# Input stage of a hybrid diffusion block: modulation products in fp32 on four column tiles over raw weights, with shift and scale panels alternating and h made by quarters

## The chip, the cores and the metric

The kernel runs on one core of one Trainium2 chip. The metric is the device time of one execution in microseconds (us). A core has a matrix engine (TensorE, PE in the rows; its weight loads are PEld), VectorE (DVE), ScalarE (ACT), GpSimd (POOL), and SyncE (SP), which here only issues transfers. ACT issues transfers as well, on a queue of its own.

## What is computed

A layer with two token mixers and a feed-forward part, on 256 context and 256 latent tokens of width 2048. Only its beginning matters here:

```python
mod_x = jax.nn.silu(c) @ lp['ada_w'] + lp['ada_b']        # ada_w: 2048 x 12288
mod_c = jax.nn.silu(c_ctx) @ lp['ada_w'] + lp['ada_b']
shx1, scx1, gx1, shx2, scx2, gx2 = [t[:, None, :] for t in jnp.split(mod_x, 6, axis=-1)]
shc1, scc1, ... = jnp.split(mod_c, 6, axis=-1)
hx = rms_norm(x, lp['norm_pre_mix']) * (1.0 + scx1) + shx1
hc = rms_norm(ctx, lp['norm_pre_mix']) * (1.0 + scc1) + shc1
px = hx @ lp['w_in']; pc = hc @ lp['w_in'][:, :MIX_IN]
```

The stage in question makes the first two of the six parts (shift and scale, 4096 columns of ada_w, 32 MB) and from them hx and hc. The other four parts are added up during the next stage, on DVE.

## The kernel before, in words

The program is a row of phases, each closed by a barrier that also clears semaphores (end_phase, L89). The first, phase_inputs (L282), ends with h ready; the second, phase_w_in (L618), multiplies h by w_in.

**Layout.** h is kept features-major, 16 feature tiles of 128 partitions by 512 tokens (context first), as two float32r parts: h_hi is h rounded, h_lo the rest. Modulation values are in modv, one column for each feature tile and each of the two vectors.

**Weights.** ada_w comes in 32 tiles of 1 MB (4 row blocks of 128 by 512 columns, sources of 2 KB each), 4 tiles to a panel of 512 columns, 8 panels. Panels 0 to 3 are the shift, 4 to 7 the scale, and they are taken in that order. raw holds four tile slots (RAW, L60). A Ring (L155) handles each tile: ACT rounds it to the high part (split_hi, L193), DVE (even tiles) or POOL (odd tiles) subtracts to get the low part (split_lo, L199), and PE multiplies both. SP loads a tile into a slot when the low part of the tile four earlier is there (L177).

**Products.** The stationary operand c_split holds silu(c) and silu(c_ctx), rounded and rest, in 4 of 128 columns, zeros in the others (L349, L388, L492, L545). The tile is the moving operand: eight products of 128x512 a tile (L473), all on the full array, added into one PSUM row block. When a panel is done, DVE copies four rows out (row, L562), PE turns them into columns with a small selector and sums the two parts (columns, L460; sel, L391), DVE copies the columns to modv (L564). Two panels make one loop body; the first two bodies are peeled, since they hold the other work.

**Other work of the stage, around the first tiles.** Four token blocks of 1 MB are loaded (L405, L417: the two x blocks reuse the ctx blocks' room), transposed on PE (turn, L434) and copied out by DVE (evac, L530). The parameters come as 25 small transfers on SP, between the ctx blocks and the first weight tile (L408), and are transposed (L448) and copied (L535). ACT stores x (L501) and squares (L504), PE adds the squares with a matrix of ones in plain fp32 (L442), DVE and ACT make 1/std (L550, L508, L552), DVE normalises in four quarters (L556).

**End of the stage.** After the last panel, DVE adds the bias to all of modv (L586), makes all gains (L589, L590), and then h is made for 16 feature tiles: ACT writes h_hi (L514), DVE the same in full into hbuf (L598), and DVE (even) or POOL (odd) subtracts (low, L365). SP prefetches the first four w_in tiles when all splits are done (L182).

Elsewhere, the scan phase has plain fp32 products of 64x64 on tiles of the array at row and column offset 0 or 64 (place, L1318; L1674, L1736, L1738).

Of the kernel before, what the change touches and what calls it, by code (L numbers as in the profile page):

```python
# [281 lines left out]
def phase_inputs(nc, A, env):  # L282
    alloc, psum, sem, Ring, col = (env[k] for k in ("alloc", "psum", "sem", "Ring", "col"))
# [3 lines left out]
    tile_no, bodies = env["tile_no"], env["bodies"]  # L287
# [27 lines left out]
    s_xt = [sem(f"i_tokens_landed{n}") for n in range(2)]  # L315
# [5 lines left out]
    s_std = sem("i_std_ready")  # L321
    s_nrm = sem("i_normalised")
# [3 lines left out]
    s_chi = sem("i_c_hi")  # L326
    s_clo = sem("i_c_split")
    s_rowc = sem("i_ada_row_copied")
    s_modp = sem("i_ada_columns_made")
    s_modc = sem("i_ada_columns_copied")  # L330
    s_v = sem("i_vector_step")
# [3 lines left out]
    s_gain = sem("i_gain_ready")  # L335
    ada = A["ada_w"].rearrange("a (k p) n -> p (a k) n", p=P)
    CW = 512
    siluc = env["siluc"]
    NB = LATE * P // CW // 2

    with ExitStack() as st:

        ring = Ring(st, "i", env["raw"], prefetched=False,
                    parts=[h.rearrange("p k t -> p (k t)").rearrange("p (s n) -> p s n", s=RAW)
                           for h in (h_hi, h_lo)])
# [3 lines left out]
        c_split = alloc(st, "c_split", [P, KT, P], f32r)  # L349
        sigc = alloc(st, "sigc", [P, 2 * KT])  # L350
        sel = alloc(st, "sel", [4, 2])
        sq = env["late_acc"][:].rearrange("p (k t) -> p k t", k=KT)
        rstd = alloc(st, "rstd", [P, TOK])
        hbuf = alloc(st, "hbuf", [P, 2, TOK])
        rows = alloc(st, "ada_rows", [4, 2, CW])
# [11 lines left out]
        tokens = [A["ctx"][0, 0:P, :], A["ctx"][0, P:2 * P, :], A["x"][0, 0:P, :], A["x"][0, P:2 * P, :]]  # L367

        with nc.Block() as block:

            @block.gpsimd
            def _(pool):
                made = [0]

                def make(ins):

                    made[0] += 1
                    ins.then_inc(s_const, 1)
                    pool.wait_ge(s_const, made[0])
# [4 lines left out]
                make(pool.memset(ones[:], 1.0))  # L384
                make(pool.memset(head_ones[:], 0.0))
# [3 lines left out]
                make(pool.memset(sel[:], 0.0))  # L389
                for base in (0, -2):  # L390
                    make(pool.affine_select(out=sel[:], in_=sel[:], compare_op=ALU.not_equal, fill=1.0, base=base,  # L391
                                            pattern=[[-1, 2]], channel_multiplier=1))

                def body(i):
                    for m in range(1, 8, 2):
                        ring.split_lo(pool, m, tile_no(i, 8, m))
                bodies(pool, NB, body, False)
                pool.wait_ge(ring.used, 8 * NB)
                for k in range(1, KT, 2):
                    low(pool, k, s_hlo)  # L400

            @block.sync
            def _(sp):
                for n in range(2):
                    sp.dma_start(xt[:, n, :], tokens[n]).then_inc(s_xt[n], 16)  # L405
                sp.wait_ge(s_const, 1)
                for tile, row, n, w, src in pieces:
                    sp.dma_start(prow[row:row + n, tile, 0:w], src).then_inc(s_prow, 16)  # L408

                def body(i):  # L410
                    for m in range(8):
                        src = ada[:, 4 * (m % 4):4 * (m % 4) + 4, bass.ds((i * 2 + m // 4) * CW, CW)]
                        ring.load(sp, src, m, tile_no(i, 8, m), (4, CW))
                        if isinstance(i, int) and i == 0 and m == 1:
                            for n in range(2, 4):
                                sp.wait_ge(s_xT, 4 * (n - 1))
                                sp.dma_start(xt[:, n % 2, :], tokens[n]).then_inc(s_xt[n % 2], 16)  # L417
                bodies(sp, NB, body, True)
                ring.prefetch(sp, 8 * NB, *first_w_in(A))
                sp.wait_ge(s_xst, 16)  # L420

            @block.tensor
            def _(pe):
                pe.wait_ge(s_const, 11)

                def turn(n):

                    pe.wait_ge(s_xt[n % 2], 16 * (n // 2 + 1))
                    for g in range(4):
# [3 lines left out]
                        for f in range(4):  # L433
                            last = pe.transpose(p_xT[b % 2][:, f * P:(f + 1) * P],  # L434
                                                xt[:, n % 2, (4 * g + f) * P:(4 * g + f + 1) * P], ident[:])
                        last.then_inc(s_xT, 1)

                def square_sums(q):
# [4 lines left out]
                    last.then_inc(s_ss, 1)  # L443
                turn(0)
                turn(1)
# [4 lines left out]
                pe.wait_ge(s_clo, 1)  # L450

                def columns(r, h):

                    pe.wait_ge(s_rowc, r + 1)
                    if isinstance(r, int) and r == 0:
                        pe.wait_ge(s_prm, 1)
                    else:
                        pe.wait_ge(s_modc, r)
                    for f in range(4):
                        last = pe.matmul(p_col[:, 2 * f:2 * f + 2], rows[:, h, f * P:(f + 1) * P], sel[:],  # L460
                                         start=True, stop=True)
                    last.then_inc(s_modp, 1)

                def body(i):
                    for h in range(2):
                        for q in range(4):
                            m = 4 * h + q
                            if q == 2 and not (isinstance(i, int) and i == 0 and h == 0):
                                columns(i * 2 + (h - 1), 1 - h)
                            ring.wait_split(pe, m, tile_no(i, 8, m))  # L470
                            for part in (ring.hi, ring.lo):
                                for k in range(4):
                                    last = pe.matmul(p_row[h][:], c_split[:, 4 * q + k, :],  # L473
                                                     part[:, m % ring.S, k * CW:(k + 1) * CW],
                                                     start=q == 0 and k == 0 and part is ring.hi,
                                                     stop=q == 3 and k == 3 and part is ring.lo)
                            last.then_inc(ring.used, 1)
                            if isinstance(i, int) and i == 0:
                                if m == 1:
                                    turn(2)  # L480
                                    turn(3)
                                if 3 <= m < 7:
                                    square_sums(m - 3)
                bodies(pe, NB, body, True)
                columns(2 * NB - 1, 1)

            @block.scalar
            def _(act):
                act.wait_ge(s_prm, 1)
                act.activation(sigc[:], prm[:, COL["c"]:COL["c"] + 2 * KT], ACT.Sigmoid).then_inc(s_sig, 1)  # L490
                act.wait_ge(s_sc, 1)
                act.activation(c_split[:, :, 0:2].rearrange("p k v -> p v k"), siluc[:], ACT.Copy)\  # L492
                   .then_inc(s_chi, 1)

                def body(i):
                    for m in range(8):
                        ring.split_hi(act, m, tile_no(i, 8, m))
                        if isinstance(i, int) and i == 0:
                            if m == 1:
                                act.wait_ge(s_fm, 16)  # L500
                                act.dma_start(xfm_d, fm[:, :, CTX:]).then_inc(s_xst, 16)  # L501
                            if 2 <= m < 6:
                                q = m - 2
                                act.activation(sq[:, 4 * q:4 * q + 4, :], fm[:, 4 * q:4 * q + 4, :], ACT.Square)\  # L504
                                   .then_inc(s_sq, 1)
                    if isinstance(i, int) and i == 0:
                        act.wait_ge(s_ssall, 1)
                        act.activation(rstd[:], rstd[:], ACT.Sqrt).then_inc(s_std, 1)  # L508
                bodies(act, NB, body, True)
                act.wait_ge(s_gain, 1)  # L510
                act.wait_ge(s_nrm, 4)
                for k in range(KT):
                    for v, lo in ((1, 0), (0, CTX)):
# [5 lines left out]
            def _(dve):  # L519
                step = [0]  # L520

                def done(ins):

                    step[0] += 1
                    ins.then_inc(s_v, 1)
# [2375 lines left out]
```

## Time and profile before

| | |
|---|---|
| median of 3 runs | 2608.91 us (2599.33 to 2609.03) |
| the profiled execution, its own time | 2605.06 us |
| its span, first to last instruction | 2603.0 us |
| busy over the span: PE, PEld, DVE, ACT, POOL | 85%, 72%, 57%, 33%, 17% |
| mean rate of all transfers over the span | 179 GB/s |
| phase_inputs, in the trace | 0 to 197.6 us |

The span is cut from the trace of one execution; the rest of its own time lies before the first and after the last instruction. Busy shares are unions of records, so records that overlap count once. A plain fp32 product leaves two PE records, a float32r product one. PEclk is the granted clock of TensorE, 1.00 for 2.4 GHz and 0.50 for 1.2 GHz.

### The profile page before, as it was taken

What the parts mean: (1) busy time and instruction counts of PE and PEld (TensorE: products, weight loads), DVE (VectorE), ACT (ScalarE), POOL (GpSimd) and SP (SyncE); (2) the same over time, 40 slices, a digit from 0 to 9 for tenths busy, and PEclk for the clock granted to TensorE, in tenths of its full rate; (3) what the DMA queues carried; (4) which work ended last, traced back from release to release, by engine and by line L of the source; (5) the groups of instructions that cost most, each with busy time, mean ns of one, the idle gap of its engine ahead of it and who ended that gap; (6) DMA issues with size and microseconds to landing.
All of it is one profiled execution on the core that took longest, in us unless ns stands there. A gap on an engine that the chain in (4) does not pass through costs nothing. (4 is left out here: it accounts for less than half of the span.)

```text
span 2603.0 us, 43450 instructions
## 1 busy us (share of the span) xinstructions
PE 2218.4 (85%) x18675; PEld 1883.0 (72%) x18675; DVE 1483.4 (57%) x1379; ACT 863.9 (33%) x878; POOL 451.2 (17%) x167
## 2 busy tenths in 40 slices
PE   6648999999799969957887839883999999989995
PEld 4437888887568857657887728773888888878884
DVE  3766666663337546667766567426655656554443
ACT  3453112111043225424433235323443333433331
POOL 3664222222103213300000014441000000000000
PEclk8778999999889989979999969996999999999996
DMA  8567888885064268854423056642555555555542
GB/s 293 183 205 273 314 314 297 319 313 139 15 194 105 77 181 276 269 110 85 76 53 75 4 196 200 202 161 96 181 192 181 189 182 189 177 194 192 197 154 105
DMA packets 438676, 465.71 MB, mean 179 GB/s; under 512 B 111822, under 2 KB 373182, under 8 KB 428798
## 3 DMA queue, kind: packets, MB, share of 16 engines
q1 hardware_dynamic: 429262, 450.23, 54.7%
q10 hardware_dynamic: 9264, 13.24, 1.4%
q8 instruction: 124, 2.03, 0.3%
q14 instruction: 26, 0.21, 0.0%
HBM read 417.69 MB, written 45.74 MB: 178 GB/s over the span
## 5 line engine op out<-in xcount | busy, mean ns | idle before, releaser
L254 PE MATMUL pf<-h,f_w_hi 128*128 128x512 f32 x1320 | 469.4, 398 | 0.0
L253 PE MATMUL pf<-h,f_w_lo 128*128 128x256 f32 x1320 | 370.2, 280 | 0.0
L199 DVE TENSOR_TENSOR f_w_lo<-t_w_raw,f_w_hi 128x2048 fp32r<-128x2048 f32 x88 | 201.4, 2289 | 173.6 <-ACT f_w_hi L193 173.6
L254 PEld LDWEIGHTS pf<-h,f_w_hi 128*128 128x128 f32 x1320 | 248.5, 188 | 56.9
L193 ACT ACTIVATE f_w_hi<-t_w_raw 128x2048 fp32r<-128x2048 f32 x88 | 168.6, 1917 | 299.1 <-PE pf L254 297.7
L253 PEld LDWEIGHTS pf<-h,f_w_lo 128*128 128x128 f32 x1320 | 249.6, 189 | 4.2
L254 PE MATMUL pd<-hid,h 128*128 128x512 f32 x688 | 244.8, 400 | 0.0
L193 ACT ACTIVATE p_w_hi<-h_w_raw 128x2048 fp32r<-128x2048 f32 (+1 forms) x54 | 98.0, 1862 | 409.1 <-DVE stage L741 252.2
L243 PE MATMUL p_in<-h,p_w_hi 128*128 128x512 f32 (+1 forms) x544 | 214.6, 395 | 19.8 <-DVE p_w_lo L199 19.8
L244 PE MATMUL p_in<-h,p_w_hi 128*128 128x512 f32 (+1 forms) x544 | 214.2, 394 | 0.0
L245 PE MATMUL p_in<-h,p_w_lo 128*128 128x512 f32 (+1 forms) x544 | 214.0, 393 | 0.0
L193 ACT ACTIVATE h<-t_w_raw 128x2048 fp32r<-128x2048 f32 x76 | 144.3, 1913 | 190.9 <-PE pd L254 150.3
L253 PE MATMUL pd<-hid,d_w_lo 128*128 128x256 f32 x688 | 193.8, 282 | 0.0
L199 POOL TENSOR_TENSOR p_w_lo<-h_w_raw,p_w_hi 128x2048 fp32r<-128x2048 f32 (+1 forms) x27 | 125.6, 4654 | 376.3 <-ACT p_w_hi L193 376.3
L871 DVE SCALAR_TENSOR_TENSOR late_acc<-h_of_x,siluc,late_acc 128x2048 f32<-128x2048 f32 x60 | 158.3, 2638 | 41.4 <-DMA h_of_x<-in_ada_w 39.8
L199 DVE TENSOR_TENSOR d_w_lo<-t_w_raw,h 128x2048 fp32r<-128x2048 f32 x44 | 100.2, 2291 | 106.6 <-ACT h L193 106.6
L254 PEld LDWEIGHTS pd<-hid,h 128*128 128x128 f32 x688 | 129.9, 189 | 31.6
L916 PE MATMUL r_pg<-h_of_x,gate_w 128*128 128x256 f32 x512 | 116.9, 386 | 20.2 <-PEq L92 12.0
L243 PEld LDWEIGHTS p_in<-h,p_w_hi 128*128 128x128 f32 (+1 forms) x544 | 100.7, 185 | 45.7 <-issue 21.3
L253 PEld LDWEIGHTS pd<-hid,d_w_lo 128*128 128x128 f32 x688 | 130.7, 190 | 0.8
L916 PEld LDWEIGHTS r_pg<-h_of_x,gate_w 128*128 128x128 f32 x512 | 99.2, 194 | 42.1 <-issue 28.6
L199 POOL TENSOR_TENSOR m_w_lo<-t_w_raw,h 128x2048 fp32r<-128x2048 f32 x8 | 40.2, 5031 | 472.6 <-ACT h L193 472.6
(438 smaller groups left out, 4486.7 us busy)
## 6 DMA issues: line engine op xcount, KB each, us to landing
h_of_x<-in_ada_w SPq DMA_DIRECT2D x64, 1024.0 KB, 5.2
h_w_raw<-in_w_in SPq DMA_DIRECT2D x48, 1024.0 KB, 7.6
t_w_raw<-in_ffn_w_gate SPq DMA_DIRECT2D x44, 1024.0 KB, 5.1
t_w_raw<-in_ffn_w_up SPq DMA_DIRECT2D x44, 1024.0 KB, 5.1
t_w_raw<-in_ffn_w_down SPq DMA_DIRECT2D x44, 1024.0 KB, 5.3
h_w_raw<-in_ada_w SPq DMA_DIRECT2D x32, 1024.0 KB, 5.7
gate_w<-in_w_in SPq DMA_DIRECT2D x32, 1024.0 KB, 5.8
t_w_raw<-in_w_out SPq DMA_DIRECT2D x16, 1024.0 KB, 5.5
```

What stands on the lines that cost most here:

```text
L193: act.activation(self.hi[:, m % self.S, 0:w], self.raw[:, s, 0:w], ACT.Copy)\
L199: eng.tensor_tensor(self.lo[:, m % self.S, 0:w], self.raw[:, s, 0:w], b32(self.hi[:, m % self.S, 0:w]), ALU.subtract)\
L243: pe.matmul(o, wh, xh, start=first, stop=False)
L244: pe.matmul(o, wh, xl, start=False, stop=False)
L245: return pe.matmul(o, wl, xh, start=False, stop=last)
L253: pe.matmul(hi, wl, x[:, 0, k, :], start=False, stop=False)
L254: return pe.matmul(both, wh, x[:, :, k, :], start=False, stop=last)
L871: dve.scalar_tensor_tensor(out=acc, in0=self.raw[:, t % 2], scalar=scalar, in1=acc, op0=ALU.mult, op1=ALU.add).then_inc(self.used, 1)
L916: mm = pe.matmul(self.banks[t % nb][:, 0:SEQ], self.raw[:, t % 2, k * P:(k + 1) * P], self.hx[:, k, :], start=k == 0, stop=k == KT - 1)
```

## The change

Products: c_cols holds the two silu vectors unrounded in 2 of 32 columns. Each of the four row blocks of a raw tile is multiplied in plain fp32 by its own 128x32 stationary block, with the output at partitions 0, 32, 64 or 96 of the same PSUM bank. Neither split is made, and a slot is free when its four products are done. The row copy takes all 128 partitions, and the selector (ones at 32g and 32g+1) adds the four groups.

Order: panels go 0, 4, 1, 5, 2, 6, 3, 7. Bias, gain and h are made for four feature tiles after each pair. All four token blocks are loaded at once (x into h_of_x), followed on SP by the weight tiles without the parameters; ACT issues the 25 parameter transfers. The w_in tiles are prefetched one by one as slots come free. PE does ctx block 0, parameters, ctx block 1, tile 0, x block 0, tile 1, x block 1, tiles 2 and 3, then a square sum after each of tiles 4 to 7; a panel's columns are made after the next panel's first tile.

```diff
-                make(pool.memset(b32(c_split[:]), 0.0))
+                make(pool.memset(c_cols[:], 0.0))
...
-                    for m in range(1, 8, 2):
-                        ring.split_lo(pool, m, tile_no(i, 8, m))
...
             def _(sp):
+                for n, (to, src) in enumerate(tokens):
+                    sp.dma_start(to, src).then_inc(s_xt[n], 16)
+                for t in range(TILES):
+                    if t >= RAW:
+                        sp.wait_ge(s_used, t - RAW + 1)
+                    at = panel(t // 4) * CW
+                    sp.dma_start(raw.slots[:, t % RAW].rearrange("p (k n) -> p k n", k=4),
+                                 ada[:, 4 * (t % 4):4 * (t % 4) + 4, at:at + CW]).then_inc(raw.landed[t % RAW], 16)
+                sources, shape = first_w_in(A)
+                for n, src in enumerate(sources):
+                    sp.wait_ge(s_used, TILES - RAW + 1 + n)
...
             def _(pe):
-                pe.wait_ge(s_const, 11)
+                pe.wait_ge(s_const, 3)
...
+                for t in range(TILES):
+                    p, q = t // 4, t % 4
+                    pe.wait_ge(raw.landed[t % RAW], 16 * (t // RAW + 1))
+                    for g in range(4):
+                        last = pe.matmul(p_row[p % 2][32 * g:32 * g + 32, :], c_cols[:, 4 * q + g, :],
+                                         raw.slots[:, t % RAW, g * CW:(g + 1) * CW], start=q == 0, stop=q == 3)
+                    last.then_inc(s_used, 1)
+                    if t < 2:
+                        turn(2 + t)
+                    if 4 <= t < 8:
+                        square_sums(t - 4)
+                    if q == 0 and p:
+                        columns(p - 1)
+                columns(PANELS - 1)
...
             def _(act):
+                act.wait_ge(s_const, 1)
+                for tile, row, n, w, src in pieces:
+                    act.dma_start(prow[row:row + n, tile, 0:w], src).then_inc(s_prow, 16)
...
                 for k in range(KT):
+                    if k % 4 == 0:
+                        act.wait_ge(s_nrm, k // 4 + 1)
+                        act.wait_ge(s_gain, k // 4 + 1)
...
             def _(dve):
+                row(0)
+                mod(0)
+                dve.wait_ge(s_ss, 4)
+                dve.tensor_scalar(rstd[:], p_ss[:], 1.0 / D, NORM_EPS, ALU.mult, ALU.add).then_inc(s_ssall, 1)
+                row(1)
+                dve.wait_ge(s_std, 1)
+                dve.reciprocal(rstd[:], rstd[:]).then_inc(s_rstd, 1)
...
+                normalised(0)
+                mod(1)
+                group(0)
+                for j in range(1, 4):
+                    normalised(j)
+                    row(2 * j)
+                    mod(2 * j)
+                    row(2 * j + 1)
+                    mod(2 * j + 1)
+                    group(j)
```

row(p) waits for the panel's last tile and copies PSUM to SBUF; mod(p) waits for the panel's columns and adds the bias into modv; normalised(j) scales a quarter of the tokens by 1/std; group(j) makes four gains and DVE's share of h for four feature tiles. columns(p) on PE waits for row(p) and mod(p-1).

## Rows read from the trace of the kernel before

**Rows 1.** Windows: busy us and instructions of each engine, granted clock, transfer share, GB/s
```profile
0.00:35.00 35.00, 19.36 (x83) 14.27 (x83) 13.61 (x23) 5.59 (x5) 8.60 (x16) 0.80 0.82 304
...
77.00:165.00 88.00, 63.75 (x228) 47.24 (x229) 67.38 (x28) 40.19 (x22) 67.70 (x12) 0.77 0.71 239
171.00:197.60 26.60, 0.00 (x0) 0.00 (x0) 23.25 (x44) 15.83 (x32) 10.77 (x8) 0.52 0.39 125
```
**Rows 2.** Waits of SP's own queue, 0 to 197.6 us: total, times, longest
```profile
SPq L179 <- DVE h L199: 72.0, 14, 16.7
SPq L179 <- POOL h L199: 51.9, 12, 6.1
```
**Rows 3.** Lines by form, 0 to 197.6 us: busy us, mean ns, idle before, releaser
```profile
L199 POOL TENSOR_TENSOR h<-h_w_raw,h 128x2048 fp32r<-128x2048 f32 x16 | 90.5, 5661 | 70.8 <-ACT h L193 70.7
L473 PE MATMUL p_row<-h,c_split 128*128 128x512 f32 x256 | 83.6, 484 | 31.8 <-DVE h L199 18.8 <-POOL h L199 13.0
L193 ACT ACTIVATE h<-h_w_raw 128x2048 fp32r<-128x2048 f32 x32 | 60.7, 1908 | 61.6 <-DMA h_w_raw<-in_ada_w 30.9 <-PE p_row L473 15.6 <-DVE fm L530 15.0
L552 DVE RECIPROCAL rstd<-rstd 128x512 f32<-128x512 f32 x1 | 3.4, 3353 | 0.7 <-ACT rstd L508 0.7
```
**Rows 4.** Windows: many transfers queued (first), one or two at a time (second)
```profile
14.00:34.00 20.00, 11.07 (x44) 8.00 (x44) 6.85 (x13) 4.30 (x4) 4.53 (x1) 0.66 1.03 397
125.00:155.00 30.00, 26.28 (x98) 19.83 (x98) 19.59 (x10) 17.23 (x9) 25.36 (x6) 0.83 0.93 317
```
**Rows 5.** Transfers by issue, whole span: count, KB each, median us to landing
```profile
h_w_raw<-in_ada_w SPq DMA_DIRECT2D x32, 1024.0 KB, 5.7
```
**Rows 6.** Timeline: start, length in us; fp32 products on full array and 64x64 tiles
```profile
49.67 3.60 PE L442 MATMUL p_ss<-late_acc,ones 128*128 128x512 f32 x8
...
1198.67 0.31 PE L1736 MATMUL pa<-vt_f,s2t_f 64*64 64x64 f32 x4
1198.79 0.31 PE L1738 MATMUL pa<-u_f,s1t_f 64*64 64x64 f32 x4
```
**Rows 7.** Windows: a stretch of the scan phase, columns as in rows 1
```profile
1180.00:1200.00 20.00, 17.60 (x585) 17.27 (x582) 15.47 (x23) 8.77 (x17) 0.00 (x0) 1.00 0.38 70
```
**Rows 8.** Timeline: the opening of the stage
```profile
1.67 0.43 SPq L408 DMA_DIRECT2D prow<-in_norm_pre_mix  x1
...
10.82 0.30 SPq L408 DMA_DIRECT2D prow<-in_gla_norm_g  x1
...
13.50 0.55 DVE L535 COPY prm<-p_col 128x384 f32<-128x384 f32 x1
...
20.91 3.75 PE L473 MATMUL p_row<-h,c_split 128*128 128x512 f32 x8 [7.73 <-DVE h L199]
...
29.16 1.04 PE L434 MATMUL p_xT<-ident,xt 128*128 128x128 f32 x8
...
34.18 1.29 DVE L530 COPY fm<-p_xT 128x512 f32<-128x512 f32 x2 [0.15 <-PE p_xT L434]
```
**Rows 9.** Timeline: a tile at either clock, a quarter normalised, one panel's columns
```profile
77.47 3.78 PE L473 MATMUL p_row<-h,c_split 128*128 128x512 f32 x8 [5.32 <-DVE h L199]
...
101.92 2.28 DVE L556 TENSOR_TENSOR fm<-fm,rstd 128x2048 f32<-128x2048 f32 x1
...
110.43 1.05 PE L460 MATMUL p_col<-sel,ada_rows 4*128 4x2 f32 x8 [1.27 <-DVE ada_rows L562]
...
111.41 2.11 PE L473 MATMUL p_row<-h,c_split 128*128 128x512 f32 x8
```
**Rows 10.** Timeline: the end of the stage
```profile
169.04 0.68 DVE L562 COPY ada_rows<-p_row 4x512 f32<-4x512 f32 x1 [4.60 <-PE p_row L473]
...
171.76 0.74 DVE L598 TENSOR_SCALAR hbuf<-fm,gain,modv 128x256 f32<-128x256 f32 x2
...
195.16 1.26 POOL L365 TENSOR_TENSOR h<-hbuf,h 128x512 fp32r<-128x512 f32 x1 [1.60 <-DVE hbuf L598]
...
197.64 0.86 SPq L858 DMA_DIRECT2D h_of_x<-in_ada_w  x2
```

More of the change, by code:

```diff
@@ L314, in phase_inputs @@
     s_prm = sem("i_params_ready")
-    s_xt = [sem(f"i_tokens_landed{n}") for n in range(2)]
+    s_xt = [sem(f"i_tokens_landed{n}") for n in range(4)]
     s_xT = sem("i_tokens_transposed")
@@ L383, in _ @@
                                         pattern=[[-1, P]], channel_multiplier=1))
+                make(pool.memset(c_cols[:], 0.0))
                 make(pool.memset(ones[:], 1.0))
+                make(pool.memset(sel[:], 0.0))
+                for g in range(4):
+                    make(pool.affine_select(out=sel[:], in_=sel[:], compare_op=ALU.not_equal, fill=1.0, base=-32 * g,
+                                            pattern=[[-1, 2]], channel_multiplier=1))
                 make(pool.memset(head_ones[:], 0.0))
@@ L403, in _ @@
             def _(sp):
[L404 to L419, printed above, removed]
+                for n, (to, src) in enumerate(tokens):
[9 more added lines that the diff above has]
+                    sp.wait_ge(s_used, TILES - RAW + 1 + n)
+                    sp.dma_start(raw.slots[:, n].rearrange("p (k n) -> p k n", k=shape[0]), src)\
+                      .then_inc(raw.landed[n], 16)
                 sp.wait_ge(s_xst, 16)
@@ L443, in square_sums, with columns @@
                     last.then_inc(s_ss, 1)
+                def columns(p):
+                    pe.wait_ge(s_rowc, p + 1)
+                    pe.wait_ge(s_modc, p)
+                    for f in range(4):
+                        last = pe.matmul(p_col[:, 2 * f:2 * f + 2], rows[:, p % 2, f * P:(f + 1) * P], sel[:],
+                                         start=True, stop=True)
+                    last.then_inc(s_modp, 1)
                 turn(0)
-                turn(1)
                 pe.wait_ge(s_prow, 16 * len(pieces))
@@ L449, in _ @@
                 last.then_inc(s_prmT, 1)
[L450 to L483, printed above, removed]
@@ L495, in body @@
[L495 to L508, printed above, removed]
@@ L531, in evac @@
                                     p_xT[b % 2][:].rearrange("p (f t) -> p f t", f=4)).then_inc(s_fm, 1)
-                for b in range(8):
+                for b in range(4):
                     evac(b)
@@ L590, in _, with row @@
-                dve.tensor_tensor(gain[:], gain[:], col("norm_pre_mix", 0, KT).unsqueeze(2)
-                                  .broadcast_to([P, KT, 2]), ALU.mult).then_inc(s_gain, 1)
-                dve.wait_ge(s_gain, 1)
-                dve.wait_ge(s_nrm, 4)
-                for k in range(KT):
-                    if k >= 2:
-                        dve.wait_ge(s_hlo if k % 2 else s_hl, k // 2)
-                    for v, lo in ((1, 0), (0, CTX)):
-                        last = dve.tensor_scalar(hbuf[:, k % 2, lo:lo + CTX], fm[:, k, lo:lo + CTX],
-                                                 gain[:, k, v:v + 1], modv[:, k, v:v + 1], ALU.mult, ALU.add)
-                    last.then_inc(s_h, 1)
-                    if k % 2 == 0:
-                        low(dve, k, s_hl)
+                def row(p):
+                    dve.wait_ge(s_used, 4 * p + 4)
+                    if p >= 2:
+                        dve.wait_ge(s_modp, p - 1)
+                    dve.tensor_copy(rows[:, p % 2, :], p_row[p % 2][:]).then_inc(s_rowc, 1)
@@ new lines, in group @@
+                def group(j):
+                    dve.wait_ge(s_modc, 2 * j + 2)
+                    at = slice(4 * j, 4 * j + 4)
+                    dve.scalar_tensor_tensor(out=gain[:, at, :], in0=modv[:, KT + 4 * j:KT + 4 * j + 4, :], scalar=1.0,
+                                             in1=col("norm_pre_mix", 4 * j, 4).unsqueeze(2).broadcast_to([P, 4, 2]),
+                                             op0=ALU.add, op1=ALU.mult).then_inc(s_gain, 1)
+                    dve.wait_ge(s_gain, j + 1)
+                    dve.wait_ge(s_nrm, j + 1)
+                    for k in range(4 * j, 4 * j + 4):
+                        if k >= 2:
+                            dve.wait_ge(s_hlo if k % 2 else s_hl, k // 2)
+                        for v, lo in ((1, 0), (0, CTX)):
+                            last = dve.tensor_scalar(hbuf[:, k % 2, lo:lo + CTX], fm[:, k, lo:lo + CTX],
+                                                     gain[:, k, v:v + 1], modv[:, k, v:v + 1], ALU.mult, ALU.add)
+                        last.then_inc(s_h, 1)
+                        if k % 2 == 0:
+                            low(dve, k, s_hl)
```

133 lines of the change are left out of this document (51 added, 82 removed).

## The prediction

> **What bounds the kernel now.** The change touches only the first stage, which ends at 197.6 us, so I read that stretch first by windows [rows 1]. Nothing in it is full. In the long middle, 77 to 165 us, PE is busy 63.75 of 88 us, DVE and POOL about 67 each, and the transfers 0.71 at 239 GB/s. From 171 us on PE does nothing at all: DVE, ACT and POOL make h. So there are two parts: a ring whose members wait for one another, and a serial tail.
>
> The waits of SP's queue say what the ring turns on [rows 2]: SP stood 72.0 + 51.9 = 123.9 us waiting for DVE and POOL to finish a low part before it could reload a slot. The lines [rows 3] give the price of one tile on each engine: ACT 1.9 us, POOL 5.7, PE 8 x 0.48 = 3.9 at mixed clock. A slot is held through landing, ACT, DVE or POOL. The transfers could go faster: with many queued they moved 397 GB/s, with the ring's one or two at a time 317 [rows 4]. A tile (1.049 MB) takes 2.64 us at the first rate and 3.31 at the second.
>
> In the tail [rows 10] 171.76 to 196.42 us, 24.66 us, goes to 16 feature tiles of h, 1.54 each, with nothing beside it, and the next stage's first issue comes 1.22 us later. What follows the barrier should keep its length, so the stage's end moves the total one for one.
>
> **The change, part by part.**
>
> *Splits removed.* 32 ACT roundings and 32 subtractions go, and with them all of the 123.9 us of waits. This gains nothing directly; it leaves two candidates for the pace, the transfers (2.64 us a tile) and PE's new products.
>
> *Products.* Four plain fp32 products of 512 columns replace eight float32r ones. The square sums are such products on the full array: four of them are 8 records in 3.60 us [rows 6], the last record's own length 0.59 included, so one record follows the next in 0.43 us, and one after another four cost 8 x 0.43 = 3.44 us. Do products on different array tiles run beside each other? The scan phase shows 64x64 ones on two diagonal tiles: groups of 4 records begin at 1198.67 and 1198.79 us, 0.12 apart, 0.029 a record [rows 6]. A record of 64 columns would need 0.43 / 8 = 0.054 us if it ran alone, so the overlap is 1.8-fold. With two tiles that is also what one gets if the two records of a product follow each other on their tile, and only the second overlaps the first record of the next product. For four tiles this gives one record time per product, 4 x 0.43 = 1.72 us a tile of weights; full overlap would give 0.86, none 3.44. I take 1.72, the pattern that the scan's row fits. The scan's tiles differ in rows too, while here all four read the same 128 partitions, each its own data; no row shows that case, hence the range and a rival.
>
> The Trainium skill (TensorE: Matmul & The Clock Gate, section on packing small matmuls) gives 2.38x for three column tiles of 32. By that alone, an estimate, four products would cost 3.44 / 2.38 = 1.45 us, the opening below would be 2 us shorter, and the total 2538.
>
> *Clock.* At 1.2 GHz all this doubles: a tile before took 3.78 us at half clock and 2.11 at full [rows 9]. 64x64 products kept 1.00 in the scan with PE busy 17.6 of 20 us [rows 7]. If the clock dropped at a transfer-bound pace, a tile would cost 3.44 us, PE would be busy all the time, and by the scan's row it should come back. I take full clock.
>
> *Start.* SP issues four token blocks and four tiles at once, 8.4 MB, 21 us at 397 GB/s. The 25 parameter transfers, 1.67 to 11.12 us on SP [rows 8], move to ACT's queue, but share the transfer engines with those 8.4 MB. Tile 0 needs silu of c, which needs them. Not delayed, they are copied at 13.5 us as before; behind everything, they land at about 25. I take 20, add 1.1 for transposing and copying and 3.5 for a token block, and start tile 0 at 24.6 us (before: 20.91 [rows 8]); both ends stay for the range, -5 and +5 us.
>
> *Opening, tiles 0 to 7.* PE does in order 8 tiles (8 x 1.72 = 13.8), two token blocks (29.16 to 35.47 less the last copy [rows 8], 2.8 each, 5.6), four square sums (4 x 3.60 = 14.4), one set of columns (1.05 [rows 9]). End: 24.6 + 34.9 = 59.4 us. Transfers are not the limit here, and storing x (2.1 MB, 5 us) fits in.
>
> *A new wait, in the middle.* DVE now does everything in order. After the square sums it needs about 5.2 us for 1/std (reciprocal alone 3.35 [rows 3]), then normalises a quarter (2.28 [rows 9]), makes bias and gain (0.4), a quarter of h (24.66 / 4 = 6.2), the next quarter's normalising (2.28) and row(2) (0.68): 59.4 + 17.0 = 76.4 us. PE reaches the columns of panel 2, after tile 12, at about 69.5 and stands there until 76.4. Queued behind that wait are tiles 13 to 16, whose slots fill meanwhile; then the transfers stop too. PE resumes at 77.5 and frees the first slot at 79.2. Later groups cost DVE 6.2 + 2.3 + 2 us in the 21 us of two panels: no such wait again, one of 1.5 us at most.
>
> *Steady run.* Tile 17, issued at 79.2, lands at about 84.2 (5.7 is the median with others in flight [rows 5]; alone I take 5). With three or four queued from here, 14 more tiles at 2.64 us: tile 31 lands at 121.2 and is used by 122.9. At 3.31 us a tile it would be 132.3. I take 397 GB/s, the row with as many queued.
>
> The Trainium skill (DMA: Bandwidth & Descriptors, specifications) puts HBM at about 358 GB/s a core, 2.93 us a tile; the total by that estimate would be 2544. The row's 397 over 20 us speaks against it.
>
> *End.* From the last product to h before: row 169.04, first h 171.76, 2.7 us, then one quarter, 6.2, and the barrier, 1.2: 10.1 us. The next stage begins at 133.0 us instead of 197.6. The four w_in tiles, issued as the last slots free, land until some 13 us after tile 31 (4 x 3.31), in time: the first is there before the stage begins, the last when its turn comes. POOL's share of h and its small work at the start lie beside DVE's.
>
> **Sum:** 197.6 - 133.0 = 64.6 us less. Against the profiled execution's own 2605.06 us: **2540**. That execution is 3.9 us under the median of 2608.91. Of the 64.6, 18.5 come from the tail (three quarters of 24.66), the rest from the ring.
>
> For this case alone the time lies between 2524 (full overlap, parameters early) and 2556 (317 GB/s, parameters late).
>
> **Rivals.**
>
> *Column tiles do not overlap,* since four streams would come out of the same 128 partitions; clock full. For it: no row shows that case. Against: the scan's 1.8. A tile costs 3.44 us and PE is the bound: opening 59.4 + 13.8 = 73.2, then 24 x 3.44 + 6 x 1.05 = 88.9, so 162.1, and with 10.1 the stage ends at 172.2, 25.4 us early: **2580**. The ring would gain little, the tail its 18.5.
>
> *Overlap as taken, but the clock stays at 1.2 GHz during these products.* 32 x 3.44 = 110.1, square sums 28.8, columns 16.8, token blocks 5.6, start 24.6: 185.9, end 196.0: **2603**, no change. Against it stands the scan's 1.00.
>
> *Slower: no overlap and half clock.* The place is L473's successor, the price 6.88 us a tile: 220.2 + 28.8 + 16.8 + 5.6 + 24.6 + 10.1 = 306.1 us, 108.5 later: **2714**. It decides from 4.2 us a tile on: (197.6 - 10.1 - 24.6 - 5.6 - 14.4 - 8.4) / 32. So even partly low clock, under 0.82 on average without overlap, makes it slower; in the middle of the ring it was 0.77 [rows 1], though there PE had gaps.
>
> *The change does not do what it says,* the splits going but the slot still waiting for something: only PE is left to wait for, which is the second case.
>
> **How the numbers follow.** Overlap and transfer-bound: 0.62. No overlap at full clock: 0.20. Overlap at half clock: 0.08. No overlap at low clock: 0.06. Something between the first two: 0.04. Faster by over 0.5% (13 us, about what can be told from no change here) is 0.62 + 0.20 + 0.04 = 0.86, same 0.08, slower 0.06. The predicted time is the likeliest case's. The range takes in that case with its bounds and the second with its own (the parameters' 5 us either way, 2575 to 2585): 2522 to 2586.
>
> **What would show it.** Right: four products a tile with PE records 0.43 us apart, two at a time; transfers near 1.0 share and 390 GB/s from tile 17 on; SP waiting for PE only; PE standing some 8 us for DVE's row(2) near 70 us; 6 us of h after the last columns; the second stage beginning near 133 us. Wrong: a tile of products at 3.4 us with PE busy throughout and SP waiting for it (no overlap), or granted clock 0.5 there; parameters landing well past 25 us; transfers at 0.9 share but 320 GB/s in spite of four slots; a second stage that is longer than before because its first tiles are late.

## The result and the profile after

| | before | after |
|---|---|---|
| median of 4 runs | 2608.97 us (2599.33 to 2610.39) | 2539.36 us (2537.36 to 2539.42) |
| ratio, 95% interval | | 0.974 (0.972 to 0.976) |
| the profiled execution, its own time | 2605.06 us | 2539.42 us |
| its span | 2603.0 us | 2537.6 us |
| first issue of phase_w_in | 197.64 us | 126.05 us |
| from there to the span's end | 2405.4 us | 2411.6 us |

69.6 us less. The prediction was 2540, 64.6 us under the profiled execution's own 2605.06, which lies 3.9 us under the median of before. The page of the kernel after, the span and the busy time of each engine:

```profile
span 2537.6 us, 43217 instructions
...
PE 2188.2 (86%) x18675; PEld 1836.9 (72%) x18675; DVE 1415.1 (56%) x1364; ACT 803.3 (32%) x845; POOL 365.1 (14%) x153
```

These shares hardly moved; the gain shows only in the stretch that the change touches. Windows of the kernel after: start and end, length, busy us of PE, PEld, DVE, ACT and POOL, granted clock, transfer share, GB/s.

```profile
15.00:35.00 20.00, 16.68 (x97) 9.32 (x98) 9.65 (x19) 4.67 (x4) 0.00 (x0) 1.00 0.99 344
35.00:50.00 15.00, 15.00 (x58) 5.98 (x57) 0.17 (x1) 4.15 (x3) 0.00 (x0) 1.00 1.06 402
65.00:75.00 10.00, 8.27 (x44) 3.50 (x44) 2.53 (x4) 0.00 (x0) 2.19 (x1) 0.58 0.56 187
80.00:110.00 30.00, 24.60 (x110) 6.78 (x102) 13.49 (x22) 4.21 (x9) 7.98 (x4) 0.51 1.04 387
```

Against the middle of the stage before, 239 GB/s [rows 1], the transfers are now the full resource (last row: 387 GB/s, 2.71 us a tile), except in a hole at 65 to 75 us. The 402 GB/s of the second row are not loads alone: 4.57 MB of loads and 1.46 MB of the store of x passed in those 15 us. Of the 24.66 us of h with PE idle at the end [rows 10] about a quarter is left. SP's waits, total, times, longest, show the ring:

```profile
SPq L405 <- PE p_row L458: 81.5, 27, 12.0
```

DVE and POOL [rows 2] are gone from it: a slot now waits for its products alone. Most of these 81.5 us are no loss, since SP waits for a slot while the other slots' transfers fill the queue; the hole at 65 to 75 us is the exception. The lines by form, 0 to 120 us: busy us, mean ns of one record, idle time before:

```profile
L458 PE MATMUL p_row<-h_w_raw,c_cols 128*32 128x512 f32 x256 | 45.7, 826 | 10.2 <-DMA h_w_raw<-in_ada_w 10.2
L442 PE MATMUL p_col<-sel,ada_rows 128*128 128x2 f32 x64 | 11.6, 304 | 9.8 <-DVE ada_rows L522 9.8
```

As many records as before, 256 [rows 3], each nearly twice as long (826 against 484 ns), and yet busy 45.7 instead of 83.6 us: they lie on top of one another. The timeline of the kernel after (start, length in us, records at the end of the line, wait before in brackets) shows the steps:

```profile
16.91 0.90 PE L448 MATMUL p_col<-ident,prow 128*128 128x128 f32 x3 [7.30 <-DMA prow<-in_gla_norm_g]
...
21.35 1.50 PE L458 MATMUL p_row<-h_w_raw,c_cols 128*32 128x512 f32 x8
...
25.41 1.07 PE L458 MATMUL p_row<-h_w_raw,c_cols 128*32 128x512 f32 x8
...
32.52 3.70 PE L434 MATMUL p_ss<-late_acc,ones 128*128 128x512 f32 x8 [0.70 <-ACT late_acc L479]
...
50.92 0.69 DVE L556 TENSOR_SCALAR rstd<-p_ss 128x512 f32<-128x512 f32 x1 [13.71 <-PE p_ss L434]
...
53.25 2.78 PE L458 MATMUL p_row<-h_w_raw,c_cols 128*32 128x512 f32 x24
57.04 1.06 PE L458 MATMUL p_row<-h_w_raw,c_cols 128*32 128x512 f32 x8 [1.01 <-DMA h_w_raw<-in_ada_w]
...
65.99 0.69 DVE L522 COPY ada_rows<-p_row 128x512 f32<-128x512 f32 x1
66.73 1.87 PE L442 MATMUL p_col<-sel,ada_rows 128*128 128x2 f32 x8 [8.62 <-DVE ada_rows L522]
68.53 6.08 PE L458 MATMUL p_row<-h_w_raw,c_cols 128*32 128x512 f32 x32
74.57 1.05 PE L442 MATMUL p_col<-sel,ada_rows 128*128 128x2 f32 x8
75.67 1.06 PE L458 MATMUL p_row<-h_w_raw,c_cols 128*32 128x512 f32 x8
79.69 1.37 PE L458 MATMUL p_row<-h_w_raw,c_cols 128*32 128x512 f32 x8 [2.95 <-DMA h_w_raw<-in_ada_w]
82.36 1.94 PE L458 MATMUL p_row<-h_w_raw,c_cols 128*32 128x512 f32 x8 [1.31 <-DMA h_w_raw<-in_ada_w]
...
115.09 1.06 PE L458 MATMUL p_row<-h_w_raw,c_cols 128*32 128x512 f32 x8 [0.81 <-DMA h_w_raw<-in_ada_w]
116.22 0.69 DVE L522 COPY ada_rows<-p_row 128x512 f32<-128x512 f32 x1 [5.35 <-PE p_row L458]
118.50 0.73 DVE L548 TENSOR_SCALAR hbuf<-fm,gain,modv 128x256 f32<-128x256 f32 x2
...
126.05 0.82 SPq L827 DMA_DIRECT2D h_of_x<-in_ada_w  x2
```

At 53.25 three tiles, 24 records, pass in 2.78 us; with the 1.06 of a tile alone that is (2.78 - 1.06) / 2 = 0.86 us for each further tile. Within the tile at 57.04, the window 57.061 to 57.45 us shows four records under way at once, the first ones of the four products:

```profile
57.04 0.64 PE L458 MATMUL p_row<-h_w_raw,c_cols 128*32 128x512 f32 x4 [1.01 <-DMA h_w_raw<-in_ada_w]
```

From 58.10 to 66.73 PE stands for DVE's copy of panel 2. From 79.69 on PE waits for a transfer before most tiles (the exceptions are the two that follow each set of columns). After the last product there is one row copy, one set of columns, one quarter of h (118.50 to about 125), and the stage is over.

### The profile page after: what moved, and what is told of

It reads as the page before. It is cut to its first block and busy times, and to the rows that moved or that the text cites. A ratio compares the mean times of both kernels' runs of the same rounds, so it can differ in the third digit from the quotient of the medians.

```text
span 2537.6 us, 43217 instructions
## 1 busy us (share of the span) xinstructions
PE 2188.2 (86%) x18675; PEld 1836.9 (72%) x18675; DVE 1415.1 (56%) x1364; ACT 803.3 (32%) x845; POOL 365.1 (14%) x153
## 5 line engine op out<-in xcount | busy, mean ns | idle before, releaser
L243 PEld LDWEIGHTS p_in<-h,p_w_hi 128*128 128x128 f32 (+1 forms) x544 | 100.8, 185 | 45.3 <-issue 20.7
L244 PEld LDWEIGHTS p_in<-h,p_w_hi 128*128 128x128 f32 (+1 forms) x544 | 100.9, 186 | 24.7
```

Of the source, the lines that this page charges most:

```text
L243: pe.matmul(o, wh, xh, start=first, stop=False)
L244: pe.matmul(o, wh, xl, start=False, stop=False)
```

## The experiments

"Stage end" is the first issue of phase_w_in in each experiment's profile; totals are medians, with the ratio to the kernel before, timed beside each. Before's median there was 2609.2 to 2610.0 us.

| run | stage end | total | ratio (95%) |
|---|---|---|---|
| e0_again, the changed kernel as it is | 125.72 | 2535.67 (one run) | |
| e1_one_tile | 169.59 | 2583.72 | 0.991 (0.988 to 0.993) |
| e2_two_tiles | 133.42 | 2550.53 | 0.978 (0.976 to 0.981) |
| e3_h_at_end | 138.16 | 2556.12 | 0.980 (0.977 to 0.983) |
| e4_row2_first | 122.75 | 2532.18 | 0.971 (0.969 to 0.974) |
| e5_two_slots | 156.60 | 2569.05 | 0.984 (0.981 to 0.988) |
| e6_params_split | 126.69 | 2540.10 | 0.975 (0.972 to 0.977) |
| e7_best | 122.03 | 2529.39 | 0.971 (0.968 to 0.973) |
| e8_changed_timed, the changed kernel | 125.63 | 2539.23 | 0.972 (0.970 to 0.974) |
| e9_best_timed, e7's kernel | 120.92 | 2533.44 | 0.971 (0.970 to 0.973) |

### How much of it is the stage, and how much scatter

> The changed kernel once more, unedited, for a second profile of it. The first stage ended at 126.05 us in the first profile; by every theory it ends within 1 us of that again. What is asked is the rest: the two profiles before and after differ by 71.6 us at the end of the first stage and by 65.4 at the end of the span. If the 6.2 us lost later are chance of the later phases' clock, the lengths of those phases move by some us here too, up or down, at the same code; if the change causes them, they repeat within 1 us of the first profile of the changed kernel.

The stage ended at 125.72 us, 0.3 from the first profile, but what follows it took 2533.9 - 125.72 = 2408.2 us, 3.4 less than in the first profile of the same code. e8 adds 2416.9, and over the ten profiles of the experiments it lies between 2404.3 and 2416.9, with no order in what was edited. The same unedited code thus spreads over 8.7 us. So the 6.2 us by which the later phases were longer after than before can't be laid to the change (there is one profile of before, 2405.4), and the stage's end is the sharper measure of an edit. What varies in the later phases no run here isolates.

### All products on one column tile

```diff
-                        last = pe.matmul(p_row[p % 2][32 * g:32 * g + 32, :], c_cols[:, 4 * q + g, :],
-                                         raw.slots[:, t % RAW, g * CW:(g + 1) * CW], start=q == 0, stop=q == 3)
+                        at = 32 * (g % 1)
+                        last = pe.matmul(p_row[p % 2][at:at + 32, :], c_cols[:, 4 * q + g, :],
+                                         raw.slots[:, t % RAW, g * CW:(g + 1) * CW],
+                                         start=q == 0 and g < 1, stop=q == 3 and g >= 3)
```

at is always 0. The row copy and the selector shrink to 32 partitions with it; the sums are the same.

> All four fp32 products of a weight tile go to the same column tile (partitions 0 to 31) and add up there; the same products, no two on different tiles. Theory (the four column tiles run at once, 0.86 us a weight tile instead of 3.44, and that moved the bound from PE to the transfers): PE becomes the bound with 8 records 0.43 us apart, 3.44 us a tile; the opening ends 8 x 2.57 = 20.6 us later, then 24 x 3.44 + 6 x 1.05, the stage ends at 171 us, the total near 2584. Rival (the gain came from leaving out the splits alone, whatever the products cost): within 5 us of 2539.

Timeline and a window of this kernel:

```profile
89.97 13.92 PE L459 MATMUL p_row<-h_w_raw,c_cols 128*32 128x512 f32 x32
103.82 1.05 PE L442 MATMUL p_col<-sel,ada_rows 32*128 32x2 f32 x8
...
169.59 0.82 SPq L829 DMA_DIRECT2D h_of_x<-in_ada_w  x2
```

```profile
80.00:160.00 80.00, 79.78 (x214) 23.21 (x212) 24.94 (x44) 10.29 (x21) 13.79 (x6) 1.00 0.88 285
```

32 records in 13.92 us, the last one 0.59 long, are (13.92 - 0.59) / 31 = 0.43 a record and 3.44 a tile, and PE is busy all of the 80 us at full clock. That is the first rival, made real: it was put at a stage end of 172.2 and a total of 2580, and came out at 169.6 and 2584. It splits the gain. Without any overlap of column tiles the stage is 28.0 us shorter than before (197.64 - 169.59), most of it the 18 us of the tail that e3 shows below; the overlap gives 43.5 more.

### Two column tiles, my price

```diff
+                        at = 32 * (g % 2)
+                        last = pe.matmul(p_row[p % 2][at:at + 32, :], c_cols[:, 4 * q + g, :],
+                                         raw.slots[:, t % RAW, g * CW:(g + 1) * CW],
+                                         start=q == 0 and g < 2, stop=q == 3 and g >= 2)
```

> The four products use two column tiles, two products on each: the price that the prediction had taken, 1.72 us a weight tile at full clock. Theory (a price under the transfers' 2.71 us a tile counts only in the opening and in the catching up after the wait for row(2)): 8 x 0.86 = 6.9 us later in the opening, about 1 more after the wait, total near 2547. Rival (at the half clock seen from 77 us on, 3.44 us a tile, PE becomes the bound from there): up to 14 x 0.73 = 10 us more, 2557.

```profile
71.66 1.86 PE L442 MATMUL p_col<-sel,ada_rows 64*128 64x2 f32 x8 [6.02 <-DVE ada_rows L524]
...
83.59 3.63 PE L459 MATMUL p_row<-h_w_raw,c_cols 128*32 128x512 f32 x16
...
91.32 1.91 PE L459 MATMUL p_row<-h_w_raw,c_cols 128*32 128x512 f32 x8 [0.78 <-DMA h_w_raw<-in_ada_w]
...
121.67 1.91 PE L459 MATMUL p_row<-h_w_raw,c_cols 128*32 128x512 f32 x8 [0.82 <-DMA h_w_raw<-in_ada_w]
...
133.42 0.82 SPq L829 DMA_DIRECT2D h_of_x<-in_ada_w  x2
```

```profile
90.00:120.00 30.00, 23.43 (x114) 7.04 (x112) 11.63 (x19) 4.04 (x8) 7.63 (x3) 1.00 1.04 386
```

Two tiles in 3.63 us put the second at 3.63 - 1.91 = 1.72: exactly the price that the prediction took for four. The stage ended at 133.42 us, the prediction said 133.0, but not because each of its terms was right. Tile 0 began at 20.52 us instead of 24.6, and PE ended the columns of panel 2 at 73.5 instead of 77.5 (predicted for the same point); from there to the end of the last product (123.58) it took 50.1 us instead of 45.4. A start four us early and a run almost five us long nearly cancel. What e2 shows without that luck is the difference: halving the price of a tile ends the stage 7.7 us earlier than here against e0 (7.4 against the first profile), since in the steady run the transfers set the pace either way (386 and 387 GB/s). The medians lie 11 us apart (2550.53 against 2539.36); the 4 us beyond the stage are within the scatter of the later phases.

### h all at the end, panels in their old order

```diff
-        return p // 2 + PANELS // 2 * (p % 2)
+        return p
...
-                group(0)
                 for j in range(1, 4):
-                    normalised(j)
                     row(2 * j)
                     mod(2 * j)
+                    normalised(j)
                     row(2 * j + 1)
                     mod(2 * j + 1)
+                for j in range(4):
                     group(j)
```

> The panels in the old order (all shift, then all scale) and all of h after the last panel; products and slots as in the changed kernel. The prediction's own term: three quarters of 24.66 us, 18.5, come back at the end. But with no h between the panels DVE is free for row(2), so the 8.6 us for which PE stood there go, of which the transfers had lost about 6.4: net 18.5 - 6.4 = 12, total near 2551. Rival (PE's stand cost nothing since the slots filled meanwhile): the whole 18.5, 2558.

```profile
65.00:75.00 10.00, 8.72 (x40) 2.59 (x40) 0.86 (x2) 0.00 (x0) 0.00 (x0) 0.50 1.04 387
```

```profile
110.00 0.69 DVE L522 COPY ada_rows<-p_row 128x512 f32<-128x512 f32 x1 [3.14 <-PE p_row L458]
...
138.16 0.82 SPq L827 DMA_DIRECT2D h_of_x<-in_ada_w  x2
```

The hole at 65 to 75 us is filled, 387 GB/s where the changed kernel had 187, and the last row copy comes 6.2 us earlier (110.00 against 116.22). Behind it lie 28.2 us instead of 9.8: 18.3 more, the 18.5 that the prediction gave to the tail. The difference is the measured 12.1. So making h in quarters earns 18 us at the end and pays 6 of them back in the middle, through the wait for row(2). The total rose by 17 us rather than 12, of which 4.6 lie in the later phases (2416.2 against 2411.6), within their scatter.

### The wait for row(2), removed

```diff
                 mod(1)
+                row(2)
                 group(0)
-                for j in range(1, 4):
...
```

DVE copies panel 2 before it makes the first quarter of h; the other steps keep their order, as row(3) and mod(3) stood ahead of group(1) already.

> DVE copies row(2) before it makes the first quarter of h; nothing else is moved. Theory (PE's stand from 58.1 to 66.7 us stops the slots being freed, and the transfers run dry): PE does not stand, tile 18 lands at 57.0 + 6 x 2.71 = 73.3 instead of 79.7 us, the stage ends 6.4 us earlier, total near 2533. Rival (the slots filled meanwhile and the run of tiles catches up): within 1.5 us of 2539.

```profile
65.00:75.00 10.00, 7.67 (x36) 2.58 (x40) 3.94 (x8) 1.50 (x4) 2.92 (x1) 0.50 1.04 387
```

```profile
58.97 1.05 PE L442 MATMUL p_col<-sel,ada_rows 128*128 128x2 f32 x8 [0.55 <-DVE ada_rows L522]
...
110.15 1.94 PE L458 MATMUL p_row<-h_w_raw,c_cols 128*32 128x512 f32 x8 [0.80 <-DMA h_w_raw<-in_ada_w]
112.90 1.86 PE L442 MATMUL p_col<-sel,ada_rows 128*128 128x2 f32 x8 [0.81 <-DVE ada_rows L522]
...
122.75 0.82 SPq L833 DMA_DIRECT2D h_of_x<-in_ada_w  x2
```

PE now waits 0.55 instead of 8.62 us for this copy, and the transfers never run dry. The last tile begins 4.9 us earlier (110.15 against 115.09), the last columns 4.1 (112.90 against 116.97), and the stage ends 3.3 earlier; 6.4 had been expected. Of the 4.9, about 1.7 go to the clock: the last tile and the last columns ran at half clock here (1.94 and 1.86 us) and at full clock in the changed kernel (1.06 and 1.08). Why the last tile came 4.9 and not 6.4 us earlier no run isolates. The median, 2532.18, is near the 2533 expected only because the later phases were short as well.

### Two slots in flight instead of four

```diff
-                    if t >= RAW:
-                        sp.wait_ge(s_used, t - RAW + 1)
+                    if t >= 2:
+                        sp.wait_ge(s_used, t - 1)
```

> SP has at most two weight tiles outstanding instead of four (it waits for two tiles back). Theory (the number queued sets the rate: 397 GB/s with many, 317 with one or two): about 3.3 us a tile instead of 2.71 in the 19 tiles of the steady run, 11 us, and some 3 in the opening, total near 2553. Rival (the memory limits the rate, whatever is queued): within 3 us of 2539.

```profile
45.00:60.00 15.00, 14.78 (x56) 4.78 (x48) 1.29 (x3) 0.45 (x1) 0.00 (x0) 1.00 0.64 212
90.00:140.00 50.00, 31.80 (x135) 9.36 (x135) 17.52 (x31) 8.08 (x16) 9.24 (x4) 0.50 0.84 274
```

The direction was as expected, the size was not: 30.5 us later instead of 14. The expectation took the 317 GB/s of [rows 4] for "two at a time"; measured were 274, and 212 beside the square sums, where a slot also waits for PE to come round. In the first of these windows the clock stood at 0.50, so that each of the two slots was also held for a tile of 1.9 us; what two slots give at full clock without the square sums was not seen. The earlier row thus was not a floor for a shallower ring. It shows how much of the gain hangs on the slots being freed early: the same products and the same order, with two slots, keep 41 of 72 us.

### Parameters earlier

```diff
                 for n, (to, src) in enumerate(tokens):
+                    if n == 2:
+                        sp.wait_ge(s_const, 1)
+                        for tile, row, rn, w, piece in pieces[1::2]:
+                            sp.dma_start(prow[row:row + rn, tile, 0:w], piece).then_inc(s_prow, 16)
```

ACT issues the other half of the 25.

> Half of the 25 parameter transfers are issued by SP between the ctx and the x blocks, the other half by ACT. Theory (25 issues one after another on one queue, then a landing behind 8.4 MB, put the parameters at 16.9 us and with them tile 0 at 21.35): they land near 11 us, tile 0 is multiplied near 16.5, the stage ends 4 to 5 us earlier, total near 2535. Rival (the opening waits for the token blocks and the first tiles, which now start 5 us later): within 1.5 us of 2539 or above.

```profile
12.81 0.90 PE L452 MATMUL p_col<-ident,prow 128*128 128x128 f32 x3 [3.27 <-DMA prow<-in_gla_norm_g]
...
19.81 1.94 PE L462 MATMUL p_row<-h_w_raw,c_cols 128*32 128x512 f32 x8 [2.49 <-DMA h_w_raw<-in_ada_w]
21.68 3.67 PE L430 MATMUL p_xT<-ident,h_of_x 128*128 128x128 f32 x16
25.28 1.06 PE L462 MATMUL p_row<-h_w_raw,c_cols 128*32 128x512 f32 x8
```

The parameters are there 4.1 us sooner (12.81 against 16.91), and the stage ends no earlier (126.69). Of the 4.1 us, PE loses 2.49 waiting for the transfer of tile 0, which begins 1.5 us earlier (19.81 against 21.35). It loses the rest to the clock: tile 0 and the x block behind it take 5.5 us (19.81 to 25.28), at record lengths of half clock, instead of 4.1 (21.35 to 25.41). So tile 1 starts only 0.13 us earlier, 25.28 against 25.41, and the wait for row(2) ends only 0.14 us earlier (66.59 against 66.73). Whether the 1.5 us would reach the stage's end at full clock no run shows.

### The waits together

e7 takes e6's split, spreads the square sums over tiles 4, 6, 8 and 10, and copies a panel's rows as soon as they are complete, inside the group of h if need be:

```diff
-                    if 4 <= t < 8:
-                        square_sums(t - 4)
+                    if t in (4, 6, 8, 10):
+                        square_sums(t // 2 - 2)
...
+                        if between and k == 4 * j + 2:
+                            row(between)
```

> Three things together: the split parameter issue; the square sums after tiles 4, 6, 8 and 10 instead of 4 to 7, so that PE frees slots at nearly the transfers' pace; and row copies set before or inside the quarters of h, so that PE never waits long for DVE. Theory (transfers are the only bound: 36 blocks of 1 MB at 2.71 us, the store of x with 5.3, 2 at the start, 105 us, last use near 106): stage end near 116, 10 us earlier, total near 2529. Rival (DVE's later 1/std makes a new wait of the same size further on): 2535 or above.

> The changed kernel unedited, timed on the same chip beside the next run, so that the two can be compared run by run. Stage end again within 1 us of 126; total near 2539, each execution within 6 us, since the part after the first stage took from 2404 to 2416 us in the nine profiles so far whatever the edit was.

> The version with the split parameter issue, spread square sums and earlier row copies, once more. Theory (its transfers are saturated from 15 us on, so it is at the floor of this volume): stage end near 122, 4 us before the changed kernel's, total some 4 to 9 us less. Rival (the 10 us of the first timing were chance of the later phases): total within 2 us of the changed kernel on this chip.

Windows and timeline of e7:

```profile
15.00:50.00 35.00, 28.17 (x143) 12.90 (x143) 9.48 (x20) 8.59 (x5) 0.00 (x0) 1.00 1.04 383
50.00:110.00 60.00, 48.43 (x244) 15.42 (x242) 33.17 (x50) 12.76 (x25) 11.81 (x6) 0.69 1.05 385
```

```profile
109.05 1.93 PE L462 MATMUL p_row<-h_w_raw,c_cols 128*32 128x512 f32 x8 [0.80 <-DMA h_w_raw<-in_ada_w]
111.80 1.86 PE L446 MATMUL p_col<-sel,ada_rows 128*128 128x2 f32 x8 [0.82 <-DVE ada_rows L526]
...
122.03 0.86 SPq L842 DMA_DIRECT2D h_of_x<-in_ada_w  x2
```

From 15 us on the transfers are full without a hole, and yet the stage ended at 122.0 and 120.9 us instead of the 116 expected. In e7 5.0 us of that miss lie before the end of the last product (110.98 instead of 106): its estimate for the volume of the transfers was too short. The end part took 11.1 us instead of 10, its first steps at half clock. That no other order of the work would gain more was not tried. The three edits together end the stage only 0.7 to 1.8 us earlier than e4, where one row copy was moved, and two runs of this same kernel differ by 1.1; most of the gain is e4's. In time, the two gave 2529.39 and 2533.44 us, the changed kernel beside the second 2539.23: 6 to 10 us less, best seen in the stage's end (4 to 5 us), while the intervals of the ratios of e8 and e9 (0.970 to 0.974, 0.970 to 0.973) overlap. That e7 met its expected total of 2529 with a stage 6 us longer than expected is the scatter of the later phases (2404.3 us here).

## Why the prediction was right

The total was met (2540 against 2539.36) and its mechanism was the one forecast: the splits go, the slot waits for PE only, the transfers become the bound, one quarter of h is left behind the last product. The precision is luck: the stage ended 7.0 us earlier than predicted (126.05 against 133.0). Against that, the sum started from an execution 3.9 us under the median, and by the medians what follows the stage was 2 us longer than before (2539.36 - 126.05 = 2413.3 against 2608.97 - 197.64 = 2411.3). So -7.0 + 3.9 + 2.0 make the miss of -1.1 us from 2540.46.

- **Overlap, the term that was mis-sized.** "For four tiles this gives one record time per product, 4 x 0.43 = 1.72 us a tile of weights"; it is 0.86. The reasoning was that two records of one product follow each other, so that only neighbours overlap. The records say otherwise: at 57.04 us the first records of all four products begin within 0.02 us, the second ones 0.43 later. Four column tiles cost what one product costs, a factor of 3.44 / 0.86 = 4.0. The scan's 1.8 came from 64-column products on two tiles, which could not show more than 2. e2 shows what the mistake was worth: 7 to 8 us of the stage.
- **No overlap, slower, half clock.** The 0.86 us a tile excludes the first rival, and e1 confirms its arithmetic. The rivals with a price of 6.88 or 3.44 us at half clock fall too: the tile at half clock took 1.94.
- **Clock.** "I take full clock" was wrong: 0.51 granted from 80 to 110 us, 1.94 us a tile. It cost nothing once the transfers set the pace, since 1.94 is below their 2.71; it did cost 1.7 us at the end of e4. The reason given, that PE would be busy all the time at half clock, rested on the doubled 1.72; with half of that PE kept gaps. That the gaps are why it stayed low is not shown (see the last section).
- **Start.** Parameters at 16.91 instead of 20, tile 0 at 21.35 instead of 24.6; within the ends that were kept. e6 shows that this term does not add up as the prediction used it: 4 us on the parameters were 1.5 on tile 0, 0.13 on tile 1 and none at the stage's end.
- **Opening.** "End: 59.4 us"; measured 50.9. Of these 8.5 us, 3.3 are the start, and eight tiles at 0.86 less would make 6.9. They sum to 10.2; 1.7 were lost again, of which 0.7 is PE's wait for the first square (32.52) and 0.6 a tile 0 partly at half clock. "Transfers are not the limit here" held for the pace: PE was busy all of the 15 us from 35 to 50 and waited for no transfer from tile 0 to tile 11 (for tile 12, 1.01 us); but the transfers were full beside it, 344, then 402 GB/s, so there was less room than the sentence says.
- **The wait in the middle.** PE "stands there until 76.4", from 69.5; measured 58.1 to 66.7. The same wait, 8.6 us instead of 6.9 (its own list of signs says "some 8"), some 10 us earlier; e3 and e4 each take it away in another way. DVE's sum of 17.0 us came out at 15.8 (50.92 to the end of the row copy, 66.68).
- **Steady run.** Predicted from the end of the wait (76.4) to the last product (122.9) 46.5 us, measured 49.4 (66.73 to 116.15). The columns took 1.80 us instead of 1.05, at half clock; from tile 13 to tile 17 it took 7.1 us instead of 6.7 (68.53 to 75.67, three tiles at half clock); tile 18 came 4.0 us after tile 17 while the queue filled again; then 13 tiles in 35.4 us are 2.72 each (2.64 predicted).
- **End.** 10.1 us predicted, 9.9 measured from the last product at 116.15 us. 18.5 from the tail: 18.3 in e3.
- **The rest.** "What follows the barrier should keep its length": nothing beyond the scatter of 2404 to 2417 us speaks against it; the ten later profiles have a mean of 2409.6 us, the one of before 2405.4.

The Trainium skill (TensorE: Matmul & The Clock Gate, section on packing small matmuls) gives 2.38x for three column tiles. It pointed the right way from the 1.8, and the trace goes beyond it: 4.0x for four fp32 tiles, 1.00 a tile where 2.38 / 3 is 0.79. In time that difference is small: even 1.72 us a tile, in e2, cost the stage only 7 to 8 us more than 0.86.

The Trainium skill (DMA: Bandwidth & Descriptors, specifications) puts HBM at about 358 GB/s a core. The trace of this program on one core disagrees, as [rows 4] had: 387 over 30 us of loads, 402 over 15 with the store of x among them. With 358 a tile would have taken 2.93 us.

## What to carry to other kernels

When a rounding or splitting step goes from a ring of loads, price the ring by the transfers' rate with all slots queued, then look for the moments at which an in-order engine (here DVE, with h before a 0.7 us row copy) holds up the engine that frees slots: those holes are what is left. Four thin plain fp32 products on four column tiles cost as one here, but past the point where PE is under the transfers' pace (here 2.7 us a tile) a cheaper product buys little (here 7 to 8 us, in the opening and in the catching up). A prediction that lands within a microsecond should still be taken apart stage by stage; here a stage that was 7.0 us short met 3.9 us from the choice of the execution it was counted from and 2 us in the later phases. An experiment that lands on a forecast deserves the same: e2 did so by two misses of over 4 us.

## What the runs showed of the hardware

- Four plain fp32 products of 128x32 by 512 columns on column tiles 0, 32, 64 and 96, each with its own moving data from the same 128 partitions, took 0.86 us together at full clock, from start to start; on one tile 3.44, on two 1.72.
- A weight tile (128x32) followed by a square sum (128x128) came every 4.63 us (41.56 to 46.19, changed kernel, full clock, PE without a gap), where 0.86 and 3.44 make 4.30; in e2 every 5.47 us (46.65 to 52.12), where 1.72 and 3.44 make 5.16. So such a pair costs about 0.3 us more than its products do among their own kind. The change of shape is the likely reason, which no run isolates.
- The granted clock was 0.51 over 30 us with PE busy 24.60 us (changed kernel), and 1.00 over 30 us with PE busy 23.43 us (e2), at 387 and 386 GB/s. The tile that kept PE at it for 1.91 us at full clock in e2 is the one of 1.06 at full and 1.94 at half clock in the changed kernel. So the same paced stretch of tiles was seen at either level. In the changed kernel the clock read 0.98 from 55 to 60 us and 0.50 from 60 to 65, after PE had stood since 58.10; in e4, where PE stood 0.55 us there, it read 1.00 and 0.54. So the clock fell without that long wait too. What lowers it was not tried.
- 1 MB tiles of 2 KB sources: 387 GB/s with four slots, 274 with two, both at half clock. After a queue ran dry, two tiles came 4.0 us apart before the pace of 2.7 was reached.
